# A hybrid decoder layer on one core: the low part of one weight chunk in each gate/up iteration made by an accumulating GpSimd DMA

## The reference, cut to what matters

```python
def hybrid_layer(x, ...):                       # x: (1, 256, 2048) float32
    h = rms_norm(x, attn_norm)
    z = h @ w_in                                # 2048 x 5184
    ... retention (6 heads), MLA attention (6 heads), gated gMLP (4 groups) ...
    y = rms_norm(concat(y_ret, y_mla, y_gm), mix_norm)
    x = x + y @ w_out                           # 2048 x 2048
    h = rms_norm(x, ffn_norm)
    return x + (silu(h @ w_gate) * (h @ w_up)) @ w_down
                                                # w_gate, w_up: 2048 x 5632, w_down: 5632 x 2048
reference = rms_norm(hybrid_layer(x), final_norm)
```

## Time and profile before

| | |
|---|---|
| median of three runs | 1125.82 us |
| profiled execution | 1125.47 us, span 1123.7 us |
| PE, DVE, ACT, GpSimd busy | 1103.9, 758.0, 571.2, 37.9 us |
| DMA | 212.42 MB, mean 189 GB/s |
| gate/up loop | about 404 to 876 us, 11 iterations of 43 us |

### The profile page before, as it was taken

One profiled execution on the slowest core, in us unless ns is written; L12 is line 12 of the kernel. 1 busy time (PEld: TensorE's weight loads), 2 busy tenths in 40 slices (PEclk: granted clock), 3 DMA queues, 4 the chain that ended last, 5 costly groups with the idle time before them and its releaser, 6 DMA issues.

```text
span 1123.7 us, 13577 instructions
## 1 busy us (share of the span) xinstructions
PE 1103.9 (98%) x5191; PEld 915.5 (81%) x5191; DVE 758.0 (67%) x674; ACT 571.2 (51%) x571; POOL 37.9 (3%) x44
## 2 busy tenths in 40 slices
PE   9999999999999999999999999999999899999997
PEld 6788889987888878888888888888888688888886
DVE  6444457655575788889888888888887544544444
ACT  6643447665755555454455454554554334333344
POOL 0380000000000000000000000000000000000000
PEclk9999999999999999999999999999999899999999
DMA  9766644644355555555555555555555455555552
GB/s 350 249 193 200 201 124 128 211 151 149 115 185 187 183 176 203 187 191 205 201 187 191 200 197 196 188 189 203 204 187 188 185 187 190 193 202 199 187 187 112
DMA packets 58315, 212.42 MB, mean 189 GB/s; under 512 B 4016, under 2 KB 11952, under 8 KB 41008
## 3 DMA queue, kind: packets, MB, share of 16 engines
q1 hardware_dynamic: 56288, 206.58, 53.6%
q10 hardware_dynamic: 2000, 5.46, 1.3%
HBM read 209.93 MB, written 2.10 MB: 189 GB/s over the span
## 4 chain that ended last, share of the span: by engine, by line
PE 84%; DMA 7%; DVE 3%; ACT 3%; issue 2%; SPq 0%; DVEq 0%; ACTq 0%
PE ps L1400 51%; PE ps L1176 9%; PE ps L1178 9%; PE ps L1177 9%; DMA raw<-in_w_gu 5%; PE ps L1215 2%; ACT w_hi L613 2%; DMA raw<-in_w_in 1%; DVE ps L1089 1%; DVE w_lo L967 1%; PE ps L1263 1%; PE ps L1364 1%; PE ps L1366 1%; PE ps L1365 1%; PE ps L1262 0%
## 5 line engine op out<-in xcount | busy, mean ns | idle before, releaser
L1400 PE MATMUL ps<-w_hi,xp_hi 128*128 128x512 f32 x539 | 213.0, 395 | 2.8 <-DVE ps L1089 2.8
L1400 PE MATMUL ps<-w_hi,xp_lo 128*128 128x512 f32 x539 | 210.1, 390 | 0.0
L1400 PE MATMUL ps<-w_lo,xp_hi 128*128 128x512 f32 x539 | 209.9, 389 | 0.0
L1095 DVE TENSOR_TENSOR w_lo<-raw,w_hi 128x2048 fp32r<-128x2048 f32 x44 | 100.8, 2292 | 119.9 <-ACT w_hi L694 119.8
L967 DVE TENSOR_TENSOR w_lo<-raw,w_hi 128x2048 fp32r<-128x2048 f32 x55 | 125.9, 2289 | 46.0 <-ACT w_hi L613 45.9
L694 ACT ACTIVATE w_hi<-raw 128x2048 fp32r<-128x2048 f32 x44 | 84.3, 1917 | 138.9 <-DMA raw<-in_w_down 138.9
L775 DVE TENSOR_TENSOR w_lo<-raw,w_hi 128x2048 fp32r<-128x2048 f32 (+2 forms) x44 | 91.9, 2088 | 88.2 <-ACT w_hi L402 88.2
L1400 PE MATMUL ps<-w_hi,dx_hi 128*128 128x512 f32 x352 | 138.2, 393 | 4.2 <-DVE ps L1144 4.2
L1400 PE MATMUL ps<-w_lo,dx_hi 128*128 128x512 f32 x352 | 137.9, 392 | 0.0
L1400 PE MATMUL ps<-w_hi,dx_lo 128*128 128x512 f32 x352 | 137.8, 392 | 0.0
L613 ACT ACTIVATE w_hi<-raw 128x2048 fp32r<-128x2048 f32 x55 | 105.0, 1910 | 62.6 <-DMA raw<-in_w_gu 62.4
(11 more groups left out here) (216 smaller groups left out, 1685.1 us busy)
## 6 DMA issues: line engine op xcount, KB each, us to landing
raw<-in_w_gu SPq DMA_DIRECT2D x88, 1024.0 KB, 4.8
raw<-in_w_down SPq DMA_DIRECT2D x44, 1024.0 KB, 4.8
raw<-in_w_in SPq DMA_DIRECT2D x34, 1024.0 KB, 5.1
raw<-in_w_out SPq DMA_DIRECT2D x16, 1024.0 KB, 5.0
raw<-in_w_in SPq DMA_DIRECT2D x8, 576.0 KB, 3.8
raw<-in_w_ukv SPq DMA_DIRECT2D x3, 1024.0 KB, 5.2
raw<-in_w_uq SPq DMA_DIRECT2D x3, 768.0 KB, 4.6
xT_raw<-in_xT SPq DMA_DIRECT2D x4, 512.0 KB, 8.1
```

What stands on the lines that cost most here:

```text
L1095: nc.vector.tensor_tensor(w_lo[n % 4][:], raw[n % 4][:], w_hi[n % 4][:].bitcast(F32), ALU.subtract).then_inc(lo_ready, 1)
L1400: mm = nc.tensor.matmul(out, x, wt, start=start and j + m == 0, stop=stop and 3 * j + m == n - 1, skip_group_check=resumed)
```

## The change

The low part of chunk p = 7 is no longer made by DVE. ACT first writes the high part as before, then the negated high part over the raw weights, in two halves (columns 0 to 1023 and 1024 to 2047 of each partition). For each half GpSimd waits, then issues a DMA that reads the same half of the chunk from HBM again and adds it to what lies in `w_lo`: -high + value = low. PE waits for both DMAs of this chunk with a semaphore of its own, and its other waits on `lo_ready` count 7 chunks for an iteration in place of 8.

```diff
+BY_DMA = (7,)
+ND = FB - len(BY_DMA)
...
 (GpSimd, after its prologue)
+            for i in range(FS):
+                for j, p in enumerate(BY_DMA):
+                    slot, row = (FF0 + p) % 4, w_gu[:, i * FB + p, :]
+                    for half in range(2):
+                        pool.wait_ge(negated, 2 * (i * len(BY_DMA) + j) + half + 1)
+                        pool.dma_start(w_lo[slot][:, 2 * half:2 * half + 2, :].rearrange("p a b -> p (a b)"),
+                                       row[:, 2 * COLS * half:2 * COLS * (half + 1)],
+                                       accum_op=ALU.add).then_inc(lo_added, 16)
...
 (ACT, prep_hi)
                     nc.scalar.activation(w_hi[slot][:], raw[slot][:], ACT.Copy).then_inc(hi_ready, 1)
+                    if p in BY_DMA:
+                        act.wait_ge(hi_ready, i * FB + (FF0 + q + 1))
+                        for half in (slice(0, 2), slice(2, 4)):
+                            nc.scalar.activation(w_lo[slot][:, half, :], w_hi[slot][:, half, :].bitcast(F32), ACT.Copy,
+                                                 scale=-1.0).then_inc(negated, 1)
...
 (DVE, prep_lo)
+                if p in BY_DMA:
+                    return
...
 (PE, ffn and down_ready)
-                    pe_.wait_ge(lo_ready, i * FB + (FF0 + p + 1))
+                    if p in BY_DMA:
+                        pe_.wait_ge(lo_added, i * (32 * len(BY_DMA)) + 32 * (BY_DMA.index(p) + 1))
+                    else:
+                        pe_.wait_ge(lo_ready, i * ND + (FF0 + sum(q not in BY_DMA for q in range(p + 1))))
...
-                pe_.wait_ge(lo_ready, i * 4 + (DN0 + k + 1))
+                pe_.wait_ge(lo_ready, i * 4 + (FF0 + FS * ND + k + 1))
```

More of the change, by code:

```diff
@@ L255, in build @@
         sum_step, tops_hi = sem("sum_step"), sem("tops_hi")
+        negated, lo_added = sem("negated"), sem("lo_added")
         mix_done, mix_first, mix_step = sem("mix_done"), sem("mix_first"), sem("mix_step")
```

## The result

The changed kernel takes 1192.86 us (median of four runs, 1191.04 to 1194.89) against 1126.62 us before (four runs here; 1125.82 was the median of the first three): a ratio of 1.0588, interval 1.0561 to 1.0614, or 66 us more. I had forecast slower, at 1144 us, with a range up to 1168. The direction was right; the loss is over three and a half times the +18 us that I had forecast. The time is outside the range.

What follows compares the result with a forecast made beforehand. TensorE, busy 98% of the span, was taken as the bound. A 2.2 us DMA wait, 1.65 us net of the mix-addition saving, times 11 gave +18: 1125.5 + 18 = 1143.5, say 1144 us; range 1118.5 to 1168.

Steps and rivals of the forecast that it cites:

- DVE loses one subtraction: On DVE, the mix addition's first half starts at part_done, so PE's eleven waits on it go: -6.0 us.
- ACT's negations cost nothing: On ACT, two added negations per iteration end at about 642.0, before its next work at 642.83: 0 us, 0.8 spare.
- Engine work, 2.67 us for a copy and twice that for an accumulate: Sixteen DMA engines' time for chunk 7's 1.05 MB: 2.67 us at 393 GB/s, doubled to 5.34 for reading old contents.
- my own upper bound: Engine work from the whole span's rate, 3.06 us for 1.05 MB: accumulate lands at 651.9, +31 us in all.
- Fixed time around the data, 1.15 + 0.5 us: Accumulating DMAs: about 1.1 us from first negation to first data, then 0.5 us from last data to a landed semaphore.
- 650.7: Forecast landing time of chunk 7's accumulate; PE, asking at 648.5, would wait 2.2 us in each iteration.
- I put nothing for it: PE's clock after its new 2.2 us wait before chunk 7: taken to stay at 1.00, 0 us.
- the single 1.8 us row: PE wait before the loop in the earlier profile that left the clock at 1.00; 2.2 us was judged nearer to it.
- much later: Rival: accumulates bound by latency land near 655; PE waits over 6 us, then half clock; some 1220 us, 7%.
- The load beside it costs nothing: SP's load issued at 643.39 ends 1.4 to 2 us later, with 6 us spare before PE uses its chunk: 0 us.
- in time: Rival: both halves move like plain loads, land by 646 before PE asks; only the -6 us remains: 1119.5 us, 38%.
- the prediction's own count of the old wait: PE's wait on the mix addition, 0.28 us in the iteration studied, cost 0.57 us there with restart; 0.55 taken on average.

Runs made afterwards that it cites:

- e1: Changed kernel without its two DMAs per iteration; PE waits for the two negations and the low part of chunk 7 stays incomplete: 1120.22 us, ratio 0.9958.
- e2: Kernel before, with only DVE's order changed: first half of the mix addition runs ahead of chunk 7's subtraction, no DMA or negation: 1120.26 us, ratio 0.9955.
- e4b: Changed kernel with both accumulating DMAs replaced by plain copies from GpSimd's queue, the addition left out: 1137.44 us, ratio 1.0114.
- e6c: Changed kernel with SP holding back the next iteration's loads of chunks 1 and 2 until both accumulating DMAs have landed: 1187.34 us, ratio 1.0566.
- e7: Changed kernel with 18 extra matmuls, never read, on PE where it would wait for the accumulating DMAs: 1173.33 us, ratio 1.0429.
- e10: e4b (plain copies) with GpSimd's descriptor space at 4096 in place of 1024: 1126.47 us, ratio 1.0029.
- e8: e6c (loads held back) with GpSimd's descriptor space at 4096 in place of 1024: 1177.93 us, ratio 1.0475.
- e3: Changed kernel with only the second half of chunk 7 by negation and accumulating DMA; DVE subtracts the first half: 1124.91 us, ratio 0.9993.
- e9: Changed kernel with GpSimd's descriptor space at 4096 in place of 1024, nothing else: 1185.69 us, ratio 1.0539.

## Why the prediction was wrong, point by point

- *DVE loses one subtraction (-6.0 us).* Right: -5.7 us in e1 and in e2, PE's eleven waits gone, the first half of the addition at part_done.
- *ACT's negations cost nothing.* Right (e1). They run back to back, as taken.
- *Engine work, 2.67 us for a copy and twice that for an accumulate.* Against SP's loads the doubling was right, 6.05 against 3.0 us by the queue table. The base was mis-sized: I took the rate of the busiest slices, and my own upper bound, the whole span's 3.06 us, was the true one. That puts the accumulate 0.7 us and the sharing 0.35 us higher. Against a plain copy by the same queue (3.5 us, e4b) the factor is only 1.7, so part of what I put down to the second read is GpSimd's queue or its smaller transfers; which of them is open. The Trainium skill (Collectives: The Full Stack, "Why ReduceScatter is half of AllGather") gives 1.93 for its own case. The two ratios here, 2.0 and 1.7, lie on either side of it.
- *Fixed time around the data, 1.15 + 0.5 us.* Too small. Without a load beside it (e6c) the pair takes 0.3 to 0.4 us from the negation to GpSimd's start and about 8.1 more to PE: 2.4 us beyond the 6.05 of engine work. That is 0.8 us more.
- Together: 650.7 + 0.7 + 0.35 + 0.8 = 652.5 in the time of the iteration that I worked with. The changed kernel has 0.3 to 0.4 and then 11.1 us behind the first negation, 641.05 + 11.5 = 652.5. PE's wait is 4.1 us by this count and not 2.2; measured are 4.35 on average and 3.6 to 4.2 without the one bad iteration.
- *Clock: "I put nothing for it".* The step that failed outright, and it hung on the one above: 4 us is the other row, the 4.24 us wait behind which the earlier trace rows showed 0.50. This is 20 us (e7). With the landing at 652.5 and nothing for the clock the sum would have given 1125.5 + 11 x 3.45 = 1163 us, inside the range. Nothing was the wrong price at 2.2 us as well. In e10 a wait of 2.15 us, and in e4b one of 2.28 us, look like this (PE's row, then the window behind it):

```profile
609.28 0.50 PE L1418 MATMUL ps<-w_hi,xp_hi 128*128 128x512 f32 x1 [2.15 <-DMA w_lo<-in_w_gu]
611.00:613.00 2.00, 2.00 (x6) 1.51 (x6) 1.58 (x1) 0.96 (x2) 0.00 (x0) 0.50 0.29 119
```

```profile
871.59 0.50 PE L1418 MATMUL ps<-w_hi,xp_hi 128*128 128x512 f32 x1 [2.28 <-DMA w_lo<-in_w_gu]
872.00:874.00 2.00, 2.00 (x10) 1.61 (x9) 1.72 (x1) 1.25 (x3) 0.00 (x0) 1.00 0.82 332
```

Of the waits of 2.2 us on the hidden rows in e6c and e8, seven of fifteen had 0.50 behind them. So a wait of this length falls either way, and the single 1.8 us row could not say that it was free. The mechanism stood in the rival "much later", tied there to a much later landing.
- *The load beside it costs nothing.* Wrong. I followed its chunk's low part to its own matmul, with 6 us spare, and not the queues behind it. By way of the gates, the sums, t_hi and the hidden rows it costs 4.0 us in e3, with only half an accumulate, and 3.9 us in e4b with plain copies. In the changed kernel's list this wait does not stand; PE comes 4 us later there.
- *Both halves go one behind the other in GpSimd's queue at once.* Not foreseen: with 1024 of descriptor space the second issue waits in five of eleven iterations until the first half has landed. In one of them (8.4 us of PE wait) this cost 4 us; otherwise nothing, because a load filled the gap.
- *The rival "in time", 1119.5 us.* It would have missed too. Plain copies, none issued late (e10), give 1126.5 us, since the loads beside them still come late and three landings of the profiled run do. A plain half takes 5.0 us to land (e4b, median, beside loads), not 3.2.

The sum over eleven iterations: PE's waits 47.9 us, lower clock 20, saved additions -6, which is 62 of the 66 us. Another 3 us are the restart, as in the prediction's own count of the old wait: from 583.45 to 587.75 PE loses 0.16 us more than the wait shows, and the matmul behind starts 0.1 us late. The rest is within the difference of single runs. Of the 48 us between +18 and +66, the later landing makes 20, the one bad iteration 4, the clock 20 and the restart 3.

## What to carry to other kernels

A DMA that adds into its destination held the DMA engines here twice as long as a load and 1.7 times as long as its own plain copy, so give it two copies' room between the loads, and look at each load whose data runs beside it: follow that one through the engines' queues, not only to its own matmul. When a forecast wait of TensorE lies between two rows of the trace with different clocks behind them, price both: here a 4 us wait cost six, and a 2.2 us wait was followed by the lower clock about every second time. And before work is moved off an engine because its queue holds something up, ask whether the held instruction can go first: two instructions exchanged on DVE gave the whole gain here (e2, 0.45%).

## What the runs showed of the hardware that I had not expected

- GpSimd takes 0.86 us for the issue of an accumulating 512 KB half and 0.53 us for a plain one; from issue to landing one half takes 5.5 us in e3, where one load's data run beside its end.
- Late second issues went from five to two with 2048 and to one with 4096, and always in the same places of the sequence, so the space given to GpSimd's descriptors has a part in whether two DMAs in a row overlap.
- All PE waits from 3.5 to 8.4 us in these runs were followed by the lower clock, 6 to 13 matmuls 0.43 us apart in the changed kernel. Of the waits of 2.0 to 2.8 us some were and some were not. One of 1.13 us (e6c) left it at 1.00, and so did the 1.8 us wait before the loop in all profiled runs but e7 and e9, where 0.50 followed. Matmuls whose result nobody reads kept it at 1.00.
